# Loading a two-layer transformer block's first inputs without waits, and copying its bias rows inside DRAM

## The reference, cut to what matters

```python
for l in range(2):                                  # first block, two layers
    u = x @ w_in[l]                                 # 1024 x 7168: conv, q, k, v (twice), gates
    y_a = conv_branch(...)                          # gated 31-tap depthwise convolution, LayerNorm, silu
    y_b = diff_attention(...)                       # 4 heads, difference of two softmaxes, lambda from lam_q, lam_k
    y_c = moba_attention(...)                       # 8 heads
    g = sigmoid(gates + b_gate[l])
    m = g[0] * y_a + g[1] * y_b + g[2] * y_c
    x = layer_norm(ALPHA * x + m @ w_o[l])
    h = square(relu(x @ w_ff1[l] + b_ff1[l]))
    x = layer_norm(ALPHA * x + h @ w_ff2[l] + b_ff2[l])
# second block, one layer: latent attention with a relative-position bias
# from rel_bias (32 buckets x 8 heads), a gated spatial unit, 32 experts, a final norm
```

## Time and profile before

| | |
|---|---|
| runs, us | 1490.9, 1486.24, 1487.67; median 1487.67 |
| profiled execution, us | 1489.11, of which the span 1487.4 |
| granted clock of PE, mean | 0.959 |
| PE busy | 1351.1 us, 91% of the span |
| DVE busy | 875.0 us, 59% |
| ACT busy | 599.7 us, 40% |
| bytes moved | 294.16 MB |

### The profile page before, as it was taken

The page is one execution under the profiler, slowest core; times in us unless marked ns, Lnnn a source line. Parts: engine busy times, 40 slices in busy tenths (PEclk is TensorE's granted clock), DMA queues, the critical chain, the costliest instruction groups (busy, mean ns, idle before and its releaser), DMA issues.

```text
span 1487.4 us, 24986 instructions
## 1 busy us (share of the span) xinstructions
PE 1351.1 (91%) x9634; PEld 1180.9 (79%) x9634; DVE 875.0 (59%) x1414; ACT 599.7 (40%) x929; POOL 34.9 (2%) x52
## 2 busy tenths in 40 slices
PE   3699998989999899999989999879799779999996
PEld 3699998979889799998969998678789656666663
DVE  2399975765555689986775555656864532221213
ACT  2235665444444344566344444434453412111111
POOL 1000000000000000000000000020140000000000
PEclk9899999999999899999999999989999869999998
DMA  7674433645556355443546555464345459999992
GB/s 219 126 237 143 157 117 102 219 154 189 195 169 197 116 188 195 142 149 100 163 132 223 183 186 195 135 203 127 117 136 194 174 208 368 391 393 380 392 394 103
DMA packets 174927, 294.16 MB, mean 198 GB/s; under 512 B 10340, under 2 KB 143092, under 8 KB 162548
## 3 DMA queue, kind: packets, MB, share of 16 engines
q1 hardware_dynamic: 170128, 285.15, 56.0%
q0 software_dynamic: 1776, 4.97, 1.4%
q10 hardware_dynamic: 2932, 2.82, 1.4%
HBM read 289.71 MB, written 3.21 MB: 197 GB/s over the span
## 4 chain that ended last, share of the span: by engine, by line
PE 65%; DVE 18%; issue 7%; ACT 5%; DMA 3%; ACTq 1%; DVEq 0%; SPq 0%
PE ps L1534 15%; PE ps L1535 14%; PE ps L1536 14%; PE ps L1915 8%; DVE w_lo L986 6%; PE ps L1901 4%; PE ps L1929 4%; ACT w_hi L624 3%; DMA raw<-in_w_in 2%; DVE cv L1102 2%; PE ps L1938 2%; ACTq L618 1%; DVE x_nat L1048 1%; DMA cv<-in_rel_bias 1%; DVE ps L1059 1%
## 5 line engine op out<-in xcount | busy, mean ns | idle before, releaser
L986 DVE TENSOR_TENSOR w_lo<-raw,w_hi 128x2048 fp32r<-128x2048 f32 (+1 forms) x170 | 378.5, 2226 | 199.6 <-ACT w_hi L624 199.0
L624 ACT ACTIVATE w_hi<-raw 128x2048 fp32r<-128x2048 f32 (+1 forms) x170 | 316.8, 1863 | 275.8 <-PE ps L1536 247.1
L1534 PE MATMUL ps<-xT_hi,w_lo 128*128 128x256 f32 (+1 forms) x1224 | 357.3, 292 | 4.1 <-DVE xT_lo L1239 2.2
L1535 PE MATMUL ps<-xT_lo,w_hi 128*128 128x256 f32 (+1 forms) x1224 | 349.6, 286 | 0.0
L1536 PE MATMUL ps<-xT_hi,w_hi 128*128 128x256 f32 (+1 forms) x1224 | 349.4, 285 | 0.0
L1534 PEld LDWEIGHTS ps<-xT_hi,w_lo 128*128 128x128 f32 (+1 forms) x1224 | 237.4, 194 | 15.1 <-issue 11.6
L1535 PEld LDWEIGHTS ps<-xT_lo,w_hi 128*128 128x128 f32 (+1 forms) x1224 | 237.4, 194 | 0.5
L1536 PEld LDWEIGHTS ps<-xT_hi,w_hi 128*128 128x128 f32 (+1 forms) x1224 | 237.0, 194 | 0.2
L1534 PE MATMUL ps<-w_hi,xT_lo 128*128 128x256 f32 (+2 forms) x560 | 172.3, 308 | 16.2 <-DVE w_lo L986 15.8
L1535 PE MATMUL ps<-w_lo,xT_hi 128*128 128x256 f32 (+2 forms) x560 | 169.5, 303 | 0.0
L1536 PE MATMUL ps<-w_hi,xT_hi 128*128 128x256 f32 (+2 forms) x560 | 169.3, 302 | 0.0
(11 more groups left out here) (334 smaller groups left out, 1943.3 us busy)
## 6 DMA issues: line engine op xcount, KB each, us to landing
raw<-in_w_in SPq DMA_DIRECT2D x72, 1024.0 KB, 5.2
raw<-in_w_ff SPq DMA_DIRECT2D x64, 1024.0 KB, 5.4
qkT<-in_w_gate SPq DMA_DIRECT2D x16, 1024.0 KB, 12.5
raw<-in_w_down SPq DMA_DIRECT2D x16, 1024.0 KB, 10.7
raw<-in_w_gate SPq DMA_DIRECT2D x16, 1024.0 KB, 13.0
w_exp<-in_w_up SPq DMA_DIRECT2D x16, 1024.0 KB, 15.2
w_exp<-in_w_down SPq DMA_DIRECT2D x16, 1024.0 KB, 11.4
raw<-in_w_o SPq DMA_DIRECT2D x8, 1024.0 KB, 5.0
```

Of the source, the lines that this page charges most:

```text
L624: nc.scalar.activation(w_hi[:, u % SPLIT, 0:n], raw[:, u % RAW, 0:n], ACT.Copy).then_inc(hi_done, 1)
L986: nc.vector.tensor_tensor(w_lo[:, u % SPLIT, 0:n], raw[:, u % RAW, 0:n], w_hi[:, u % SPLIT, 0:n].bitcast(F32), ALU.subtract).then_inc(spli ...
L1534: nc.tensor.matmul(out_, left[1], right[0], start=start, stop=False)
L1535: nc.tensor.matmul(out_, left[0], right[1], start=False, stop=False)
```

## The change

- x is loaded in two halves, each with a semaphore. SP issues both, then units 0 to 3 with no wait for the constants. After unit 3's load it issues the six parameter arrays and then the rotary tables, the mask, `t5` and `rel_bias`, and after these unit 4's load.
- ACT issues the identity matrix alone. It rounds unit 0, then makes x's transposed halves, then rounds unit 1.
- POOL waits for unit 1 before its six broadcasts.
- PE transposes x as soon as the identity and a half of x are there. It transposes the parameters after unit 1 and does the t5 matmul after unit 2, in other PSUM banks.
- DVE does its small set-up operations at units 4 and 7 instead of before the loop.
- ACT stores the 8 bias rows once, 16 KB, to a new DRAM tensor `z_row`. POOL waits for that and copies it 128 times over to `z_dram`, from DRAM to DRAM.
- `rel_bias` gets another place in on-chip memory, in `lnb`; its load of the layer-norm rows on SP now waits for `z_row_in`.
- The two layers are written out: `for l in range(LAYERS)` in Python in place of `Fori`, on SP, ACT, DVE and PE. Waits are on constants. Loops inside the feed-forward part stay.

```diff
-CONSTS, BCASTS = 11 * 16, 6 * 16
-
-ACT_LINKS, DVE_LINKS = 1, 93
+PARAMS, CONSTS, BCASTS = 6 * 16, 4 * 16, 6 * 16
...
-        relb = cv[0:32, 0, 0:N_HEADS]
+        relb = lnb[0:32, 2, 512:512 + N_HEADS]
...
+        z_row = nc.dram_tensor("z_row", (N_HEADS, 512), F32, kind="Internal").ap()
...
-            sp.dma_start(x_nat[:], t["x"].rearrange("o (a p) d -> p (o a) d", p=P)).then_inc(x_in, 16)
+            for a in range(TT):
+                sp.dma_start(x_nat[:, a, :], t["x"].rearrange("o (a p) d -> p (o a) d", p=P)[:, a, :]).then_inc(x_in[a], 16)
...
-            with sp.Fori(0, LAYERS) as l:
+            for l in range(LAYERS):
                 base = l * UNITS
                 for u in range(U_BR):
-                    if u == 2:
-                        sp.wait_ge(const_in, CONSTS)
+                    if (l, u) == (0, RAW):
+                        for dst, src in ((row_cw, t["conv_w"].rearrange("l k o (c p) -> (k o c) l p", p=P)),
+                                         (row_v[C_CB:C_CG], t["conv_b"].rearrange("l (c p) -> c l p", p=P)),
+                                         (row_v[C_CG:C_CBT], t["conv_ln_g"].rearrange("l (c p) -> c l p", p=P)),
+                                         (row_v[C_CBT:C_GB], t["conv_ln_b"].rearrange("l (c p) -> c l p", p=P)),
+                                         (row_v[C_GB:C_F1], t["b_gate"].rearrange("l (c p) -> c l p", p=P)),
+                                         (row_v[C_F1:C_CW], t["b_ff1"].rearrange("l (c p) -> c l p", p=P))):
+                            sp.dma_start(dst, src).then_inc(prm_in, 16)
+                        for dst, src in ((rot[:], t["c_rot"].rearrange("k (a p) d -> p k a d", p=P)), (mask[:], t["c_mask"]), (t5, t["c_t5"]), (relb, t["rel_bias_2"])):
+                            sp.dma_start(dst, src).then_inc(const_in, 16)
                     load(base, u, unit3(raw, u % RAW, KC, 256), w_in[:, bass.ds(l * KC, KC), COLS_OF[u] * 256:(COLS_OF[u] + 1) * 256])
...
-                        sp.wait_ge(z_stored, 16)
+                        sp.wait_ge(z_row_in, 16)
...
+            pool.wait_ge(raw_in[1], 16)
             for i, name in enumerate(("lam_q1", "lam_k1", "lam_q2", "lam_k2")):
                 pool.dma_start(lamv[:, i, :], t[name].rearrange("l d -> (l d)").partition_broadcast(P)).then_inc(bcast_in, 16)
...
+            pool.wait_ge(z_row_in, 16)
+            pool.dma_start(z_dram.ap(), bc(z_row, 1, P)).then_inc(z_stored, 16)
...
-            for dst, src in ((ident[:], t["c_ident"]), (mask[:], t["c_mask"]),
...
-                             (t5, t["c_t5"]), (relb, t["rel_bias_2"])):
-                act.dma_start(dst, src).then_inc(const_in, 16)
+                act.wait_ge(act_link, links[0])
+
+            act.dma_start(ident[:], t["c_ident"]).then_inc(ident_in, 16)
...
-            act.dma_start(z_dram.ap(), bc(t5_row, 1, P)).then_inc(z_stored, 16)
-            act.wait_ge(lam_sum, 1)
-            nc.scalar.activation(lams[:], lams[:], ACT.Exp).then_inc(lam_exp, 1)
-
-            with act.Fori(0, LAYERS) as l:
...
+            act.wait_ge(raw_in[0], 16)
+            hi(0, 0)
+
+            for l in range(LAYERS):
+                base = l * UNITS
...
                 make_xT(0)
-                nc.scalar.activation(prm[:], prm_all[:, bass.ds(l, 1), :].rearrange("p o c -> p (o c)"), ACT.Copy).then_inc(prm_cur, 1)
-                act.wait_ge(prm_cur, l + 1)
+                if l == 0:
+                    act.wait_ge(raw_in[1], 16)
+                    hi(0, 1)
+                else:
+                    nc.scalar.activation(prm[:], prm_all[:, l, :], ACT.Copy).then_inc(prm_cur, 1)
+                    act.wait_ge(prm_cur, l + 1)
...
+                    if (l, u) == (0, 1):
+                        act.wait_ge(setup_mm, PRM_ROWS)
...
+                        act.wait_ge(setup_c, PRM_ROWS)
+                        nc.scalar.activation(prm[:], prm_all[:, l, :], ACT.Copy).then_inc(prm_cur, 1)
+                        act.wait_ge(prm_cur, l + 1)
+                    if (l, u) == (0, 2):
+                        act.wait_ge(setup_mm, T5_ROW)
+                        nc.scalar.activation(t5_row, ps[0:N_HEADS, O_B, :], ACT.Copy).then_inc(setup_c, 1)
+                        act.wait_ge(setup_c, T5_ROW)
+                        act.dma_start(z_row, t5_row).then_inc(z_row_in, 16)
+                    if (l, u) == (0, 5):
+                        act.wait_ge(lam_sum, 1)
+                        nc.scalar.activation(lams[:], lams[:], ACT.Exp).then_inc(lam_exp, 1)
...
-            dve.wait_ge(setup_p, 2)
-            dve.wait_ge(const_in, CONSTS)
-            dve.wait_ge(bcast_in, BCASTS)
...
-
-            with dve.Fori(0, LAYERS) as l:
...
+
+            for l in range(LAYERS):
+                base = l * UNITS
...
                 make_xT(0)
                 split(base, 1)
-                dve.wait_ge(prm_cur, l + 1)
                 for u in range(U_BR):
+                    if u == 2:
+                        dve.wait_ge(prm_cur, l + 1)
+                    if (l, u) == (0, 1):
+                        dve.wait_ge(setup_p, 2)
+                    if (l, u) == (0, 4):
+                        dve.wait_ge(const_in, CONSTS)
+                        dve.wait_ge(bcast_in, BCASTS)
+                        pairs = lamv[:].rearrange("p (a b) d -> p b a d", b=2)
+                        link(nc.vector.tensor_tensor(pairs[:, 0], pairs[:, 0], pairs[:, 1], ALU.mult))
+                        nc.vector.tensor_reduce(lams[:], pairs[:, 0].rearrange("p a (l d) -> p a l d", l=LAYERS), AX.X, ALU.add).then_inc(lam_sum, 1)
+                        for i in range(LAYERS):
+                            nc.vector.tensor_scalar(gsub[:, i, :], gsub[:, i, :], linit[:, 1, i:i + 1], None, ALU.mult)
+                    if (l, u) == (0, 7):
+                        dve.wait_ge(lam_exp, 1)
+                        link(nc.vector.tensor_tensor(nlam[:], lams[:, 1, :], lams[:, 0, :], ALU.subtract))
+                        link(nc.vector.tensor_tensor(nlam[:], nlam[:], linit[:, 0, :], ALU.subtract))
...
-            pe.wait_ge(const_in, CONSTS)
...
-
-            nc.tensor.matmul(ps[0:N_HEADS, 6, :], relb, t5, start=True, stop=True).then_inc(setup_mm, 1)
-            pe.wait_ge(setup_p, 2)
-            pe.wait_ge(x_in, 16)
-            pe.wait_ge(setup_c, PRM_ROWS)
+            pe.wait_ge(ident_in, 16)
             pe.sem_inc(x_out, X_CREDIT)
 
             xT = (xT_hi, xT_lo)
-            with pe.Fori(0, LAYERS) as l:
+            for l in range(LAYERS):
...
-                make_xT(0)
+                if l == 0:
+                    for a in range(TT):
+                        pe.wait_ge(x_in[a], 16)
+                        for c in range(KC):
+                            last = nc.tensor.transpose(ps[:, ACC + c // 2, (c % 2) * T + a * P:(c % 2) * T + (a + 1) * P], x_nat[:, a, c * P:(c + 1) * P], ident[:])
+                            if a == TT - 1 and c % 2 == 1:
+                                last.then_inc(xT_done, 1)
+                else:
+                    make_xT(0)
...
+                    if (l, u) == (0, 1):
+                        pe.wait_ge(prm_in, PARAMS)
+                        for i in range(LAYERS):
+                            nc.tensor.transpose(ps[:, TB, i * 256:i * 256 + C_CW], row_v[:, i, :], ident[0:C_CW, 0:C_CW])
+                            last = nc.tensor.transpose(ps[:, TB, i * 256 + C_CW:i * 256 + C_ALL], row_cw[:, i, :], ident[0:CONV_W * CC, 0:CONV_W * CC])
+                        last.then_inc(setup_mm, 1)
+                    if (l, u) == (0, 2):
+                        pe.wait_ge(const_in, CONSTS)
+                        nc.tensor.matmul(ps[0:N_HEADS, O_B, :], relb, t5, start=True, stop=True).then_inc(setup_mm, 1)
+                    if (l, u) == (0, 5):
+                        pe.wait_ge(setup_c, T5_ROW)
+                        pe.wait_ge(setup_p, 2)
```

More of the change, by code:

```diff
@@ L277, in build @@
         evac_a, evac_d = sem("evac_a"), sem("evac_d")
-        const_in, bcast_in, x_in, lnb1_in, lnb2_in = sem("const_in"), sem("bcast_in"), sem("x_in"), sem("lnb1_in"), sem("lnb2_in")
+        ident_in, prm_in, z_row_in = sem("ident_in"), sem("prm_in"), sem("z_row_in")
+        const_in, bcast_in, x_in, lnb1_in, lnb2_in = sem("const_in"), sem("bcast_in"), [sem(f"x_in{a}") for a in range(TT)], sem("lnb1_in"), sem("lnb2_in")
         setup_p, setup_mm, setup_c, lam_sum, lam_exp = sem("setup_p"), sem("setup_mm"), sem("setup_c"), sem("lam_sum"), sem("lam_exp")
@@ L698, in _ @@
                         last.then_inc(evac_a, 1)
+                    if (l, u) == (0, 1):
+                        act.wait_ge(setup_mm, PRM_ROWS)
+                        rows_v = ps[:, TB, :].rearrange("p (l c) -> p l c", l=LAYERS)
+                        for a, b, scale in ((C_CB, C_CG, 1.0), (C_CG, C_F1, 0.5), (C_F1, C_ALL, 1.0)):
+                            last = nc.scalar.activation(prm_all[:, :, a:b], rows_v[:, :, a:b], ACT.Copy, scale=scale)
```

(25 more changed lines are left out.)

87 lines of the change are left out of this document (26 added, 61 removed).

## The result

The changed kernel takes **1462.0 us** (median of 4 runs, 1460.12 to 1462.45); the kernel before took 1487.4 beside it. The ratio is 0.982, interval 0.981 to 0.983: 25.4 us faster. The forecast was 1476; what came is rival (a) with 1460. The profiled execution took 1461.86 us, of which the span is 1459.8 (before 1487.4, so -27.6).

The account below looks back on a forecast made before the run. PE was taken as the bound, with two holes: a late start and a weight stall after unit 4. 1489.1 - 14.2 + 1.4 - 15.0 + 16.0 = 1477.3, or 1476 us against the median; own range 1471 to 1482, with rival (a) 1457 to 1483.

Parts of the forecast that it names:

- rival (a): Bias-row copy to z_dram: fast, since eight source partitions were the cause; no stall, 1460 us; chance 0.33.
- I take the target as the cause: 0.287 stays: Copy to z_dram: its DRAM target is what is slow, so packets keep 0.287 us (bounds 0.086 to 0.57).
- So the stall comes back, later: Copy from about 41.5 to 84 us delays weights: unit 9 nearly 2 us late, unit 10 12.5 late.
- +16: Sum's term for PE's returning stall at units 9 and 10, including 1.5 us for its restart at 1.2 GHz.
- a fast beginning looks like buffers filling: Old bias store: packets of 0.086 us in its first 1.45 us, then 0.287, taken to show a slow target.
- the output's stores: Evidence against a slow target: output stores write 3.6 KB packets in 0.144 us, so DRAM takes writes fast.
- The start: -14.2: Program start: PE's first product at 14.1 us instead of 28.32; bounds -15.5 to -8.
- cold start: PE in unit 0: adds 1.1 us to the unit's end, at 21.0 us.
- The moved PE stream: +1.4: Four parameter transposes and t5 matmul between PE's units: 0.45 + 0.93 us warm, all on the path; bounds 1.4 to 2.8.
- the 18 to 20 I took: SP's moved loads: SP held until 18 to 20 us, unit 4's load landing by 28, needed at 33.
- The second hole: -15.0: PE idle 14.52 us after unit 4; removal brings layer 0's 475.7 us to layer 1's 460.7.
- Layers written out: 0: Hardware loop over layers replaced: no gain or cost, bounds -3 to +1; layer 1 stays at 460.7 us.

Follow-up runs that it names:

- e1: Changed kernel with the old store back: ACT writes the 8 bias rows 128 times into z_dram from on-chip memory after unit 2; 1477.77 us, ratio 0.9937.
- e3: Changed kernel with the copy inside DRAM to z_dram issued by ACT after unit 3 in place of POOL; 1460.02 us, ratio 0.9815.
- e5: Changed kernel with ACT's store from on-chip SBUF again, its eight source rows 16 partitions apart; 1459.52 us, ratio 0.9809.
- e9: Changed kernel with ACT's store from on-chip SBUF again, its eight source rows 2 partitions apart; 1458.9 us, ratio 0.9803.
- e4: Kernel before with only the bias rows' new way: stored once to z_row, then copied inside DRAM by POOL; 1471.22 us, ratio 0.9894.
- e10: Kernel before with only the two layers written out in place of the hardware loop; 1485.16 us against 1488.82, ratio 0.9979.
- e2: Changed kernel with z_dram written from on-chip memory (SBUF) by POOL's queue; 1483.3 us, ratio 0.9969.
- e8: Changed kernel with unit 0 of layer 0 loaded, rounded and split in halves, x's transposed parts made between them; 1458.76 us, ratio 0.9798.
- e11: Changed kernel with unit 0's load issued ahead of x's two halves; 1455.78 us, ratio 0.9787.
- e12: The e8 version with the first half of unit 0 issued ahead of x and the second behind it; 1455.13 us, ratio 0.978.

## Why the prediction was wrong

**The step that failed.** "I take the target as the cause: 0.287 stays", and with it "So the stall comes back, later", the term **+16**. Measured: 0.160 us for 4 KB, no late unit, 0. With e1 that term measures 479.42 - 461.86 = 17.6 us; the size was nearly right for a store that was no longer there. e3 changes only the source and gets 0.084 us; e5 and e9 change only the distance of the source partitions and halve the packet. The target and the queue are excluded as what made the packet slow. Rival (a) named the cause, eight source partitions (in fact eight neighbouring ones), and its 1460 came, 2 us from the measured 1462.0.

**Why I chose wrongly.** I weighed one row, 93 packets at 0.086 us in the first 1.45 us, as "a fast beginning looks like buffers filling". In e1 the same store shows no such beginning. Its queue in the first 1.5 us of the store, 39.5 to 41:

```profile
q10 hardware_dynamic: 40, 0.08, 47.0%
```

That is 0.470 x 16 x 1.5 / 40 = 0.282 us per packet at once. So the fast beginning doesn't belong to the store, and an argument on it could not bear half of the chance. What it was stays open. The row that I set against it, the output's stores at 0.144 us for 3.6 KB into DRAM, was the better one: it measured the disputed resource itself.

**The start: -14.2.** Measured -13.6: `w_hi` at 9.74 instead of 9.2, first product at 14.72 instead of 14.1. The chain unit 0, `w_hi`, `w_lo`, `xT_lo` was right.

**What the start left out.** I counted a cold start (the first products at 1.2 GHz) of 1.1 us into unit 0's end and not into the sum. It costs 2.4 us in the changed kernel, by the distances of its first 25 products. The kernel before has nine such products, 28.32 to 30.34: 2.02 - 9 x 0.12 = 0.9 us. The difference of 1.5 us had no place in the sum.

**The moved PE stream: +1.4.** Four transposes between 28.67 and 29.18 and the matmul pair of 1.02 us: 0.5 + 1.0, as said. Nothing waited for the parameters at unit 1. `conv_w`, `conv_b` and the mask each held SP for 2.7 to 2.9 us, and it was free for unit 4 at 20.99, a little later than the 18 to 20 I took; unit 4 was not late. (`conv_ln_g`, of the same shape as `conv_b`, held it for 0.30 us; what makes the difference is not shown.)

**The second hole: -15.0.** e4 gives -16.0 in medians, and in its profiled execution the stretch from first product to end of layer 0 is 485.77 - 27.11 = 458.66 us, 17.1 less than before. My yardstick, layer 1 of before, carried the low clock behind its layer norm (0.63), 2.3 us that layer 0 doesn't have: 15.0 + 2.3 = 17.3. In this are the 0.9 us of slow first products of the kernel before, which e4 doesn't have; the hole alone is some 16 us. With the stream and the changed kernel's cold start, -17.1 + 1.4 + 2.4 = -13.3 against -13.9 measured for layer 0; 0.6 us stays without a cause. My terms without the stall give 1.4 - 15.0 = -13.6. That they come so near is luck: two misses, 2.1 and 2.4 us, cancelled.

**Layers written out: 0.** -0.1 in layer 1 of the two traces, both with the low clock. By itself it was worth 3.1 +/- 1.4 us (e10), at or beyond the end of my bounds. In the changed kernel's profiled execution, whose layer 1 drew the low clock, the other terms leave at most the 0.6 us of layer 0 for it.

## What to carry to other kernels

When a transfer has two peculiar ends, put a chance on each from rows that measure that end by itself, and not from how a transfer of both begins. A store that replicates a few rows is better fed from DRAM or from partitions that aren't neighbours; look at us per packet, not only at the number of engines. When two inputs meet in the first product, issue first the one with the longer chain behind it, and see that PE's first work, here the transposes, runs straight into the products.

## What the runs showed of the hardware

- Eight neighbouring SBUF partitions as the source of a store to DRAM gave 0.298 us per 2 KB packet on ACT's queue and 0.623 per 4 KB on POOL's: 53 to 55 GB/s for eight engines together. With the eight 2 or 16 partitions apart it was 0.139 and 0.155 per 2 KB, from DRAM 0.084, from 128 partitions on 16 engines 0.094.
- POOL's queue merged two 2 KB rows into one 4 KB packet, at 0.160 us from DRAM. In e2 such packets, as slow per byte as e1's, went with a weight unit that took 44.0 us to land instead of 38.0.
- The granted clock right behind a layer norm differs between executions, 0.60 to 0.63 or 0.88 to 0.91, and moves the time by 2.2 to 2.3 us. Differences of that size need the stretch's clock beside them.
- At the start of the program the column of the granted clock can read 1.00 while matmuls follow each other in 0.21 us instead of 0.12 (e8, e11 to 12.79). The gap between x's transposes and the first product was 5.35 us with 25 slow products behind it, 2.07 with 28 (e8), 0.23 with six (e11) and 0.32 with none (e12).
